# Pairs of SwiGLU chunks computed with seven products: four pairs in two rows of two in place of three single ones

## The chip, the cores and the metric

The kernel runs on one core of a Trainium2 chip. The metric is the device time of one execution in microseconds (us); less is better.

## What is computed

Two transformer blocks, one after the other, on 256 rows of 1024 features in fp32. The first block has an adaLN modulation, attention beside a convolution, and a squared-ReLU MLP with 4096 hidden features. The second has two attention branches and a SwiGLU MLP with 2816 hidden features (`D_FF_2`), 11 chunks of 256:

```python
def second_block(x, norm_mix, w_in, w_up_a, w_up_b, w_out, norm_ffn, w_gate, w_up, w_down, norm_final):
    ...
    x = x + merged @ w_out[layer]
    h = rmsnorm(x, norm_ffn[layer])
    x = x + (jax.nn.silu(h @ w_gate[layer]) * (h @ w_up[layer])) @ w_down[layer]
    return rmsnorm(x, norm_final)
```

The change touches the line with `silu`, and what is prepared for it earlier.

## The kernel before, in words

**Precision.** A product in fp32 is made of three fp32r products: of an operand, the high part H is its rounding to fp32r and the low part L the rest. PE runs H x WH, H x WL and L x WH into one bank (`part`, lines 570 to 572). A *unit* is 1 MB of weights, 128 x 2048, brought by one or two DMAs of SP's queue into one of seven slots `W32[0..6]`. ACT writes its high halves WH (`hi()`, line 1247, two instructions for a unit) and DVE its low halves WL (`lo()`, line 1791, two instructions). WL lies in the same bytes as W32. Both engines go through all units in one order, that of the list `units`; SP loads them in the order of `loads`. The queue of every engine is written out by hand, and an engine that waits holds up what stands behind it.

**The SwiGLU MLP.** The 256 rows are two blocks of 128 (`tb`), the 1024 features two halves. For one chunk, PE makes gate and up side by side, 256 + 256 columns (`up2`), for each `tb` two units of 12 matmuls. ACT takes the silu, DVE multiplies with up into `hid` (line 1800), PE transposes it (`hid_turn2`), ACT and DVE split it into HH and HL, and PE adds its product with w_down in banks 0 to 3 (`down2`). `GROUPS` lists chunks and pairs of chunks; `PAIRS = (2, 5, 8)` makes pairs of 2 and 3, 5 and 6, 8 and 9, and chunks 0, 1, 4, 7 and 10 are single.

**A pair.** Here gate and up of 512 columns for two row blocks and two halves of the features are a 2 x 2 product of blocks, made with seven products of 12 matmuls in place of eight. Four of the seven have a sum of blocks of x as one operand (`FS`, split into `FH` and `FL`; formed once by `form`, `form_hi`, `form_lo`) and four a difference of weight blocks. PE runs them in the order 1 to 7 (`begin`, `rest`, `quad_sum`): 1 (bank 4), 2 (bank 5), the down products of the group before for one `tb`, 3 (bank 6), those for the other `tb`, 4 (bank 5), 5 (bank 6), 6 (bank 4), 7 (bank 6). Between them DVE adds up banks and earlier sums (*first* to *fifth sum*, `quad_group` in `vector_program`; they write `g1b` and `quad_g1`), each raising the semaphore `quad`. The fourth product waits for the first sum, the fifth for the second and the seventh for the third, because the bank must have been read:

```python
        w.wait_ge(S["quad"], 5 * q + 2)
        quad_sum(g, 4, 3, 6, False)
        ...
        w.wait_ge(S["quad"], 5 * q + 3)
        part(by["gu", g][6], m.AH, m.AL, 4, 1, 6, False, True, "gu_mm", n_ready(2, 1), onto=True)
```

**Weight differences.** They come in two ways. *In place* (pairs not in `STORED`): DVE subtracts one unit in its slot from another (`make(g, 0)` to `make(g, 3)`, two instructions of 1024 elements each), before their low halves are made. *Stored*: four steps bring a quarter of the up and gate blocks each into a free place in SBUF (POOL, `blocks_in`), DVE makes the four differences (`kept_sums`, four instructions of 512 elements), and POOL writes them to DRAM (`kept_sums` in `pool_program`), from where SP later loads them as units. `STEPS` says how many steps there are in each of three phases and `SUMS_AT` at which place of DVE's queue they stand: places 0 to 6 are in the first block's MLP, 7 in the projections of the second block. Before, pair 2 is stored and pairs 5 and 8 are in place. `DN_ORDER`, `GU_AT`, `QUAD_AT` and the like turn the order into the semaphore values that the waits use.

## Time and profile before

| | |
|---|---|
| median of 3 runs | 718.48 us (718.40 to 718.58) |
| the profiled execution | 718.42 us |
| its span in the profile | 716.3 us |
| PE busy | 706.7 us, 99% |
| DVE busy | 574.6 us, 80% |
| ACT busy | 429.9 us, 60% |
| DMA | 163.76 MB, 229 GB/s |
| the SwiGLU MLP | from about 541 us to the end |

Start times in the trace are from the start of the span. The time of an execution is 2.1 us over its span. Ends of matmuls are modelled and overlap the next start, so PE's pace is read from start to start. In the rows, "x4" merges four instructions of one kind, and the brackets give the idle time of the engine before them and what ended it.

### The profile page before, as it was taken

What the parts mean: (1) busy time and instruction counts of PE and PEld (TensorE: products, weight loads), DVE (VectorE), ACT (ScalarE), POOL (GpSimd) and SP (SyncE); (2) the same over time, 40 slices, a digit from 0 to 9 for tenths busy, and PEclk for the clock granted to TensorE, in tenths of its full rate; (3) what the DMA queues carried; (4) which work ended last, traced back from release to release, by engine and by line L of the source; (5) the groups of instructions that cost most, each with busy time, mean ns of one, the idle gap of its engine ahead of it and who ended that gap; (6) DMA issues with size and microseconds to landing.
All of it is one profiled execution on the core that took longest, in us unless ns stands there. A gap on an engine that the chain in (4) does not pass through costs nothing.

```text
span 716.3 us, 9684 instructions
## 1 busy us (share of the span) xinstructions
PE 706.7 (99%) x3710; PEld 565.7 (79%) x3710; DVE 574.6 (80%) x972; ACT 429.9 (60%) x704; POOL 34.5 (5%) x55
## 2 busy tenths in 40 slices
PE   8999999999999999999999999999999999999996
PEld 4678885578888888888888777777888888888885
DVE  4789999899677868686998799855857789888883
ACT  3477658996745635646545677767447654754652
POOL 1030012001100100000010000000000000000000
PEclk9999999999999999999999999999999999999999
DMA  9996939617778975747538533336463894976901
GB/s 368 414 374 222 389 102 358 230 59 262 272 246 311 337 281 203 258 154 291 164 113 295 209 118 118 118 130 214 128 234 128 315 329 169 332 258 227 354 2 59
DMA packets 72109, 163.76 MB, mean 229 GB/s; under 512 B 4272, under 2 KB 15536, under 8 KB 70528
## 3 DMA queue, kind: packets, MB, share of 16 engines
q1 hardware_dynamic: 68016, 149.47, 58.8%
q0 software_dynamic: 3760, 13.42, 5.2%
q8 instruction: 29, 0.48, 0.3%
q10 hardware_dynamic: 288, 0.27, 0.1%
q14 instruction: 16, 0.13, 0.1%
HBM read 157.90 MB, written 5.24 MB: 228 GB/s over the span
## 4 chain that ended last, share of the span: by engine, by line
PE 95%; issue 1%; DVE 1%; ACT 1%; POOL 0%; POOLq 0%; DVEq 0%
PE bank L570 23%; PE bank L572 23%; PE bank L571 23%; PE bank L915 6%; PE bank L552 5%; PE bank L913 3%; PE bank L589 1%; PE bank L644 1%; PE bank L652 1%; PE bank L647 1%; PE bank L1047 1%; PE bank L1069 1%; PE bank L753 1%; PE bank L629 1%; PE bank L775 1%
## 5 line engine op out<-in xcount | busy, mean ns | idle before, releaser
L1791 DVE TENSOR_TENSOR WL<-W,WH 128x1024 fp32r<-128x1024 f32 (+2 forms) x240 | 270.4, 1172 | 25.6 <-ACT WH L1247 25.2
L1247 ACT ACTIVATE WH<-W 128x1024 fp32r<-128x1024 f32 (+2 forms) x240 | 228.6, 1013 | 63.4 <-DMA W<-in_w_mlp 38.1
L570 PE MATMUL bank<-WH,AHL 128*128 128x512 f32 (+1 forms) x420 | 165.2, 393 | 0.0
L572 PE MATMUL bank<-WH,AHL 128*128 128x512 f32 (+1 forms) x420 | 162.0, 386 | 0.0
L571 PE MATMUL bank<-WL,AHL 128*128 128x512 f32 (+1 forms) x420 | 161.8, 385 | 0.0
L570 PEld LDWEIGHTS bank<-WH,AHL 128*128 128x128 f32 x420 | 78.9, 188 | 18.2 <-issue 3.2
L572 PEld LDWEIGHTS bank<-WH,AHL 128*128 128x128 f32 x420 | 78.9, 188 | 16.2
L571 PEld LDWEIGHTS bank<-WL,AHL 128*128 128x128 f32 x420 | 79.1, 188 | 14.7
L570 PE MATMUL bank<-WH,HH 128*128 128x512 f32 (+1 forms) x218 | 84.8, 389 | 0.0
L572 PE MATMUL bank<-WH,HL 128*128 128x512 f32 (+1 forms) x218 | 84.5, 388 | 0.0
L571 PE MATMUL bank<-WL,HH 128*128 128x512 f32 (+1 forms) x218 | 84.4, 387 | 0.0
L915 PE MATMUL bank<-AHL,WH 128*128 128x512 f32 x168 | 60.5, 398 | 0.0
L913 PE MATMUL bank<-AHL,WL 128*128 128x256 f32 x192 | 50.0, 281 | 0.0
L572 PEld LDWEIGHTS bank<-WH,HL 128*128 128x128 f32 x218 | 40.9, 188 | 8.5
L571 PEld LDWEIGHTS bank<-WL,HH 128*128 128x128 f32 x218 | 41.0, 188 | 8.3
L570 PEld LDWEIGHTS bank<-WH,HH 128*128 128x128 f32 x218 | 40.9, 188 | 8.0
L913 PEld LDWEIGHTS bank<-AHL,WL 128*128 128x128 f32 x192 | 36.3, 189 | 2.0
L915 PEld LDWEIGHTS bank<-AHL,WH 128*128 128x128 f32 x168 | 31.6, 188 | 6.7
L1806 DVE SCALAR_TENSOR_TENSOR cacc<-hp,vec,cacc 128x256 f32<-128x256 f32 x88 | 36.0, 478 | 0.2
L436 POOL TENSOR_TENSOR stat<-stat 128x1 f32<-128x1 f32 x12 | 10.1, 845 | 444.3 <-DVE stat L1815 401.8
L1255 ACT ACTIVATE HH<-bank 128x512 fp32r<-128x512 f32 (+1 forms) x20 | 8.9, 487 | 24.4 <-PE bank L552 24.4
L1800 DVE TENSOR_TENSOR W<-W,W 128x1024 f32<-128x1024 f32 x16 | 18.8, 1215 | 0.0
(311 smaller groups left out, 978.5 us busy)
## 6 DMA issues: line engine op xcount, KB each, us to landing
W<-in_w_mlp SPq DMA_DIRECT2D x32, 1024.0 KB, 5.9
W<-in_w_in SPq DMA_DIRECT2D x24, 1024.0 KB, 5.5
W<-in_w_down SPq DMA_DIRECT2D x11, 1024.0 KB, 5.3
W<-in_w_ada SPq DMA_DIRECT2D x10, 1024.0 KB, 8.3
WX<-in_w_ada SPq DMA_DIRECT2D x10, 1024.0 KB, 10.2
W<-in_w_up SPq DMA_DIRECT2D x9, 1024.0 KB, 6.2
W<-in_w_out SPq DMA_DIRECT2D x8, 1024.0 KB, 5.3
W<-in_w_gate SPq DMA_DIRECT2D x8, 1024.0 KB, 5.8
```

The costliest lines, as they stand in the source:

```text
L436: e.tensor_tensor(m.stat[:, 40 + i:41 + i], m.stat[:, 24 + i:25 + i], m.stat[:, 94:95], ALU.pow).then_inc(S["rstd"], 1)
L552: ins = e.transpose(bank[b][:, c * 128:c * 128 + 128], src, m.ident[:, :])
L570: e.matmul(po, hs, wh[:, k, c0:c0 + cw], start=first and k == 0, stop=False, skip_group_check=onto)
L571: e.matmul(po, hs, wl[:, k, c0:c0 + cw], start=False, stop=False, skip_group_check=onto)
L572: ins = e.matmul(po, ls, wh[:, k, c0:c0 + cw], start=False, stop=last and k == unit.nk - 1, skip_group_check=onto)
L913: ins = e.matmul(bank[4 + j][:, 0:256], wl[:, k, js], m.AH[:, 4 * i + k, :], start=False, stop=False)
L915: ins = e.matmul(both, wh[:, k, js], m.AHL[:, :, 4 * i + k, :], start=False, stop=i == 1 and k == 3)
L1247: e.activation(m.WH[unit.slot][:, c], m.W32[unit.slot][:, c], ACT.Copy).then_inc(S["w_hi"], 1)
L1255: e.activation(o, i, ACT.Copy, scale=scale).then_inc(S[sem], 1)
L1791: e.tensor_tensor(m.WL[unit.slot][:, c], m.W32[unit.slot][:, c], m.WH[unit.slot][:, c].bitcast(F32), ALU.subtract).then_inc(S["w_lo"], 1)
L1800: e.tensor_tensor(o, a, b, op).then_inc(S[sem], 1)
L1806: e.scalar_tensor_tensor(o, a, scalar, b, op0, op1).then_inc(S[sem], 1)
```

## The change

- `PAIRS` becomes (2, 4, 7, 9): the pairs (2, 3), (4, 5), (7, 8) and (9, 10), with 0, 1 and 6 single. There is one group fewer (`NG` is 7). The first pair of each two in a row is made in place, the second is stored.
- Eight steps of stored sums in place of four: one at each of places 0 to 6 (the first phase of POOL), one at place 7 (the second).
- `NEAR` lists pairs that another pair follows. In them ACT and DVE split two units of the next pair ahead of time, in a new order within the group (`quad_group` in both programs).
- The last group is a pair; PE moves half of the down products of the pair before behind its seventh product, and `down2_last` has two units.

```diff
-PAIRS = (2, 5, 8)
-STORED = (2,)
-STEPS = (4, 0, 0)
-SUMS_AT = (1, 0, 1, 0, 0, 0, 2, 0, 0, 0, 0, 0, 0)
+PAIRS = (2,4,7,9)
+STORED = (4,9)
+STEPS = (7,1,0)
+SUMS_AT = (1,1,1,1,1,1,1,1,0,0,0,0,0)
...
+NEAR = [g for g in range(NG - 1) if GROUPS[g][1] and GROUPS[g + 1][1]]
...
     def down2_last():
...
+        g = NG - 1
         for n, (c0, cw) in enumerate(LAST[1]):
-            part(by["dn", NG - 1][0], m.HH[(NG - 1) % 2], m.HL[(NG - 1) % 2], 0, 1, (1, 4, 5)[n], n > 0, True, "dn_mm",
-                 lambda k: ("hid_lo", 16 + 2 * NG), c0, cw)
+            for i, unit in enumerate(by["dn", g]):
+                part(unit, m.HH[g % 2], m.HL[g % 2], 2 * i, 1, (1, 4, 5)[n], n > 0 and i == 0, i == 1, "dn_mm",
+                     lambda k: ("hid_lo", 16 + 2 * NG), c0, cw)
...
         quad_sum(g, 2, 1, 6, True)
-        down2(g - 1, 1, False, False)
+        if g < NG - 1:
+            down2(g - 1, 1, False, False)
         w.wait_ge(S["quad"], 5 * q + 1)
...
+    rest(NG - 1)
+    hid_turn2(NG - 1, 0)
     down2(NG - 2, 1, False, False, (0,))
     down2(NG - 2, 1, False, True, (1,))
+    down2(NG - 1, 0, False, True, (0,))
+    hid_turn2(NG - 1, 1)
+    down2(NG - 1, 0, False, True, (1,))
     down2_last()
```

On ACT, in `quad_group`, and on DVE, in `quad_group` (the bodies of the named steps are as before):

```diff
-        hi(5)
-        hi()
+        near, final = g in NEAR, g == NG - 1
+        hi(4 if g - 1 in NEAR else 5)
+        hi(2 if near else 1)
...
         if made:
             make(g, 2)
         lo()
+        if g == 2:
+            form_lo(2)
+            form_lo(3)
+        first_sum()
         if made:
             make(g, 3)
         lo()
...
         if near:
+            lo()
+            second_sum()
+            lo(4)
+            third_sum()
+            fourth_sum()
+            lo()
+            hidden(0)
+            fifth_sum()
+            lo()
+            hidden(1)
             hid_lo2(g, 0)
+            hid_lo2(g, 1)
...
+        else:
+            second_sum()
+            lo(2)
+            third_sum()
             lo()
+            fourth_sum()
...
```

**DVE at the opening of pair (2, 3).** The first row multiplies the second row block of chunk 0 with its silu (`hid0`), the last is the low part of chunk 1's hidden rows or just before it. `W32_n` is slot n, `WL_n` and `WH_n` its low and high halves, FL the low parts of the sums of x, HL those of the hidden rows. Before:

```order
L1800 TENSOR_TENSOR hid0_164<-bank5,rel1_171 128x256
L2126 TENSOR_TENSOR HL0_168<-bank7,HH0_166 128x2x128
L1791 TENSOR_TENSOR WL_5_60<-W32_5_54,WH_5_66 128x1024 x2
L1791 TENSOR_TENSOR WL_2_57<-W32_2_51,WH_2_63 128x1024 x2
L1800 TENSOR_TENSOR hid1_165<-bank1,rel1_171 128x256
L2126 TENSOR_TENSOR HL0_168<-bank6,HH0_166 128x2x128
L1800 TENSOR_TENSOR FL0_220<-FS0_216,FH0_212 128x512
L1800 TENSOR_TENSOR FL1_221<-FS1_217,FH1_213 128x512
L1800 TENSOR_TENSOR FL2_222<-FS2_218,FH2_214 128x512
L1800 TENSOR_TENSOR FL3_223<-FS3_219,FH3_215 128x512
L1791 TENSOR_TENSOR WL_3_58<-W32_3_52,WH_3_64 128x1024 x2
```

and with the change:

```order
L1799 TENSOR_TENSOR hid0_164<-bank5,rel1_171 128x256
L2125 TENSOR_TENSOR HL0_168<-bank7,HH0_166 128x2x128
L1799 TENSOR_TENSOR W32_2_51<-W32_2_51,W32_5_54 128x1024 x2
L1790 TENSOR_TENSOR WL_5_60<-W32_5_54,WH_5_66 128x1024 x2
L1799 TENSOR_TENSOR hid1_165<-bank1,rel1_171 128x256
L2125 TENSOR_TENSOR HL0_168<-bank6,HH0_166 128x2x128
L1799 TENSOR_TENSOR W32_3_52<-W32_3_52,W32_2_51 128x1024 x2
L1799 TENSOR_TENSOR FL0_220<-FS0_216,FH0_212 128x512
L1799 TENSOR_TENSOR FL1_221<-FS1_217,FH1_213 128x512
L1790 TENSOR_TENSOR WL_2_57<-W32_2_51,WH_2_63 128x1024 x2
L1790 TENSOR_TENSOR WL_0_55<-W32_0_49,WH_0_61 128x1024 x2
L2125 TENSOR_TENSOR HL1_169<-bank7,HH1_167 128x2x128
```

Two makes (W32_2 and W32_3 as outputs) have come in, and the low passes of slots 2 and 0 stand behind them; FL2 and FL3 have moved back.

**DVE from there to the third quad sum of pair (2, 3).** The rows that read bank5 or bank6 into g1b are the first, second and third sum. Before:

```order
L2126 TENSOR_TENSOR HL1_169<-bank7,HH1_167 128x2x128
L2126 TENSOR_TENSOR HL1_169<-bank6,HH1_167 128x2x128
L1791 TENSOR_TENSOR WL_0_55<-W32_0_49,WH_0_61 128x1024 x2
L1800 TENSOR_TENSOR g1b_74<-bank5,quad_g1_228 128x512
L1791 TENSOR_TENSOR WL_1_56<-W32_1_50,WH_1_62 128x1024 x2
L1800 TENSOR_TENSOR g1b_74<-bank6,quad_g1_228 128x512
L1791 TENSOR_TENSOR WL_4_59<-W32_4_53,WH_4_65 128x1024 x2
L1791 TENSOR_TENSOR WL_5_60<-W32_5_54,WH_5_66 128x1024 x2
L1800 TENSOR_TENSOR g1b_74<-bank6,g1b_74 128x512
```

and with the change (ahead of these rows stand the second HL1 row, the make of W32_1 and the low pass of slot 3):

```order
L1799 TENSOR_TENSOR FL2_222<-FS2_218,FH2_214 128x512
L1799 TENSOR_TENSOR FL3_223<-FS3_219,FH3_215 128x512
L1799 TENSOR_TENSOR g1b_74<-bank5,quad_g1_228 128x512
L1799 TENSOR_TENSOR W32_5_54<-W32_4_53,W32_5_54 128x1024 x2
L1790 TENSOR_TENSOR WL_4_59<-W32_4_53,WH_4_65 128x1024 x2
L1790 TENSOR_TENSOR WL_5_60<-W32_5_54,WH_5_66 128x1024 x2
L1799 TENSOR_TENSOR g1b_74<-bank6,quad_g1_228 128x512
L1790 TENSOR_TENSOR WL_6_210<-W32_6_209,WH_6_211 128x1024 x2
L1790 TENSOR_TENSOR WL_1_56<-W32_1_50,WH_1_62 128x1024 x2
L1790 TENSOR_TENSOR WL_2_57<-W32_2_51,WH_2_63 128x1024 x2
L1790 TENSOR_TENSOR WL_3_58<-W32_3_52,WH_3_64 128x1024 x2
L1799 TENSOR_TENSOR g1b_74<-bank6,g1b_74 128x512
```

Between the first and the second sum there is a make and two low passes where there was one low pass; between the second and the third there are four low passes where there were two.

## Rows read from the trace of the kernel before

**Rows 1.** The page, busy us (share of the span) of all engines, instructions.

```profile
PE 706.7 (99%) x3710; PEld 565.7 (79%) x3710; DVE 574.6 (80%) x972; ACT 429.9 (60%) x704; POOL 34.5 (5%) x55
```

**Rows 2.** The page, the chain that ended last, by engine.

```profile
PE 95%; issue 1%; DVE 1%; ACT 1%; POOL 0%; POOLq 0%; DVEq 0%
```

**Rows 3.** Windows: stretch, its length, busy us of each engine (instructions), granted clock, DMA.

```profile
564.00:592.00 28.00, 28.00 (x127) 23.20 (x126) 21.52 (x23) 19.00 (x21) 0.00 (x0) 1.00 0.94 343
612.00:640.00 28.00, 28.00 (x129) 23.24 (x128) 24.83 (x26) 19.03 (x22) 0.00 (x0) 1.00 0.96 339
```

**Rows 4.** Timeline of PE in pair (2, 3): start, us, line, op; fourth, sixth, seventh product.

```profile
575.31 0.39 PE L570 MATMUL bank<-WH,FH 128*128 128x512 f32 x1
...
580.75 0.39 PE L570 MATMUL bank<-WH,AHL 128*128 128x512 f32 x1
...
583.47 0.39 PE L570 MATMUL bank<-WH,AHL 128*128 128x512 f32 x1
```

**Rows 5.** Timeline of DVE, pair (2, 3); in brackets the idle time before.

```profile
551.79 0.42 DVE L2126 TENSOR_TENSOR HL<-bank,HH 128x256 fp32r<-128x256 f32 x1
552.67 4.63 DVE L1791 TENSOR_TENSOR WL<-W,WH 128x1024 fp32r<-128x1024 f32 x4 [0.46 <-ACT WH L1247]
557.22 0.42 DVE L1800 TENSOR_TENSOR hid<-bank,rel 128x256 f32<-128x256 f32 x1
...
557.88 2.49 DVE L1800 TENSOR_TENSOR FL<-FS,FH 128x512 fp32r<-128x512 f32 x4
...
566.20 2.36 DVE L1791 TENSOR_TENSOR WL<-W,WH 128x1024 fp32r<-128x1024 f32 x2 [2.90 <-ACT WH L1247]
...
572.79 0.69 DVE L1800 TENSOR_TENSOR g1b<-bank,quad_g 128x512 f32<-128x512 f32 x1 [1.35 <-PE bank L572]
...
580.95 0.69 DVE L1800 TENSOR_TENSOR g1b<-bank,g1b 128x512 f32<-128x512 f32 x1 [2.93 <-PE bank L572]
```

**Rows 6.** SP's issue of a load; the page's median us from issue to landing.

```profile
547.30 0.34 SPq L409 DMA_DIRECT2D W<-sums  x1
...
W<-in_w_up SPq DMA_DIRECT2D x9, 1024.0 KB, 6.2
...
W<-sums SPq DMA_DIRECT2D x4, 1024.0 KB, 5.1
```

**Rows 7.** Timeline of DVE, pair (5, 6), first to third quad sum.

```profile
616.14 0.68 DVE L1800 TENSOR_TENSOR g1b<-bank,quad_g 128x512 f32<-128x512 f32 x1
616.74 2.35 DVE L1800 TENSOR_TENSOR W<-W,W 128x1024 f32<-128x1024 f32 x2
619.01 2.35 DVE L1791 TENSOR_TENSOR WL<-W,WH 128x1024 fp32r<-128x1024 f32 x2
621.28 0.68 DVE L1800 TENSOR_TENSOR g1b<-bank,quad_g 128x512 f32<-128x512 f32 x1
...
628.60 0.69 DVE L1800 TENSOR_TENSOR g1b<-bank,g1b 128x512 f32<-128x512 f32 x1 [2.10 <-PE bank L572]
```

**Rows 8.** Timeline of PE, pair (5, 6), start of the seventh product.

```profile
631.12 0.39 PE L570 MATMUL bank<-WH,AHL 128*128 128x512 f32 x1
```

**Rows 9.** Timeline of DVE in the first MLP: a step of sums, a wait.

```profile
232.34 2.62 DVE L1800 TENSOR_TENSOR sums<-sums 128x512 f32<-128x512 f32 x4
...
259.24 2.36 DVE L1791 TENSOR_TENSOR WL<-W,WH 128x1024 fp32r<-128x1024 f32 x2 [4.90 <-ACT WH L1247]
```

**Rows 10.** Timeline of PE, first and last of the 12 narrow matmuls.

```profile
708.75 0.28 PE L570 MATMUL bank<-WH,HH 128*128 128x256 f32 x1
...
710.06 0.28 PE L572 MATMUL bank<-WH,HL 128*128 128x256 f32 x1
```

**Rows 11.** Windows after the last matmul; the granted clock is behind the engines.

```profile
711.00:714.00 3.00, 0.00 (x0) 0.00 (x0) 1.29 (x4) 1.14 (x3) 0.54 (x1) 1.00 0.02 8
714.00:715.00 1.00, 0.00 (x0) 0.00 (x0) 0.00 (x0) 0.00 (x0) 0.00 (x0) 0.83 1.02 389
715.00:716.30 1.30, 0.00 (x0) 0.00 (x0) 0.00 (x0) 0.00 (x0) 0.00 (x0) 0.50 0.26 93
```

More of the change, by code:

```diff
@@ L474, in kept_sums @@
             s = sum(STEPS[:phase]) + i
+            if phase == 2 and i == 1:
+                power(10)
             w.wait_ge(S["made"], 4 * s + 4)
@@ L1713, in quad_group @@
         e.activation(m.rel[1][:, :], m.g1[:, :], ACT.Silu).then_inc(S["silu"], 1)
-        if not GROUPS[g + 1][1]:
+        if near:
+            hi()
+            hid_hi2(g, 0)
+            hi()
+        elif not final:
             hi(2)
-        for tb in range(2):
-            hid_hi2(g, tb)
-        if GROUPS[g + 1][1]:
-            hi(2)
+            hid_hi2(g, 0)
+        hid_hi2(g, 1)
     silu_gate(0, 0)
@@ L2563, in quad_group, with product, first_sum, second_sum @@
         q = quads.index(g)
-        made, following, near = in_place(g), in_place(g + 1), GROUPS[g + 1][1]
+        made, near, final = in_place(g), g in NEAR, g == NG - 1
+        following = not final and in_place(g + 1)
+        def product(n):
+            w.wait_ge(S["gu_mm"], QUAD_AT[g] + n)
+        def first_sum():
+            product(2)
+            w.wait_ge(S["quad_act"], q + 1)
+            if q:
+                w.wait_ge(S["hid2"], HID_AT[quads[q - 1], 1])
+            tt(m.u1, bank[5][:, :], m.g1[:, :], ALU.add, "quad")
+        def second_sum():
+            product(3)
+            tt(m.u0, bank[6][:, :], m.g1[:, :], ALU.add, "quad")
+        def third_sum():
+            product(5)
+            tt(m.u1, bank[6][:, :], m.u1, ALU.add, "quad")
+        def fourth_sum():
+            product(4)
+            w.wait_ge(S["quad"], 5 * q + 2)
+            tt(m.u0, bank[5][:, :], m.u0, ALU.add, "quad")
+        def fifth_sum():
+            product(7)
+            tt(m.g1[:, :], bank[6][:, :], m.g1[:, :], ALU.add, "quad")
+        def hidden(tb):
+            w.wait_ge(S["hid_turned"], 4 + 2 * (g - 2) + 2)
+            w.wait_ge(S["silu"], SILU_AT[g, tb])
+            w.wait_ge(S["quad"], 5 * q + 4)
+            tt(m.hid[g % 2][:, tb, :], (m.u0, m.u1)[tb], m.rel[tb][:, :], ALU.mult, "hid2")
         if made:
@@ L2661, in vector_program @@
                 hid_lo2(g, tb)
[L2662 to L2666 removed]
+    quad_group(NG - 1)
     def last(tb):
```

127 lines of the change are left out of this document (42 added, 85 removed).

## The prediction

> **What bounds the kernel now.** I read the busy shares first: PE is busy for 706.7 of 716.3 us and DVE for 80% of it [rows 1]. Then the chain of waits: 95% of it is PE, and no other engine has over 1% [rows 2]. So a microsecond of PE work is worth a microsecond, and work on another engine costs nothing until PE waits for it. The stage windows show how near that is: PE fills all of 564 to 592 and of 612 to 640 at a granted clock of 1.00, while DVE has 21.5 and 24.8 us of 28 to do [rows 3]. Last I read the queues of PE and DVE side by side there, because DVE works in the order in which it is written, and that order is what the change rewrites.
>
> A product (12 matmuls of 512 columns) takes PE 2.72 us: the fourth of pair (2, 3) starts at 575.31, the sixth 24 matmuls later at 580.75, the seventh at 583.47 [rows 4]. That is 0.2267 us for a matmul. From start to start, an FL row takes DVE 0.60 us (four rows from 557.88 with 2.49 us to the last end) and a small row of 256 elements 0.33 us (two from 557.22 to 557.88) [rows 5]. A quad sum takes 616.14 to 616.74, 0.60 us; a difference of two weight blocks (two W rows, "a make") 616.74 to 619.01, 2.27 us; a low pass (one unit, two WL rows) 619.01 to 621.28, also 2.27 us [rows 7].
>
> **What it removes.** The fourth pair makes 7 products of what were 8. In matmuls of the whole program it is 18 fewer of 512 columns and 12 more of 256, since the narrow last rows now have two units. The first and the last of the 12 there now start at 708.75 and 710.06, so they come 0.119 us apart [rows 10]. 18 x 0.2267 - 12 x 0.119 = **-2.65 us** of PE, all on the path. PE's tail after its last matmul keeps its form: 0.
>
> **Sums kept in DRAM, eight steps in place of four.** A step is four DVE rows, 2.6 us [rows 9]. The added ones stand at the end of a chunk of the first MLP, where DVE idles: in one of them it waits 4.90 us before the low pass at 259.24 [rows 9], and in each chunk it waits for ACT or PE somewhere. The block that they delay is used by PE a chunk later. POOL's added copies (eight loads of half a unit, four stores) are queued behind nothing that PE needs; the last of the first seven is issued before the power of the next norm, as now. The eighth, in the second block's projections, delays DVE by 2.6 us ahead of ropes and relu rows for which it waits on ACT. I cost all of it at nothing; if that cover were gone it would be at most 2.6 us for a step. Extra DMA: 8 MB through the sums and 3 MB of units. I count 0 to 1 us for both.
>
> **DVE's queue in pair (2, 3), the first place.** Before, this pair is stored, so DVE has no makes in it. It waits for others four times between 552.13 and the third sum: 0.46, 2.90, 1.35 and 2.93 us [rows 5]. Now the pair is made in place, so four makes stand there, and because another pair follows, four low passes stand between the second and the third sum in place of two, and one more before the second. The order of both places is shown above. I add it up from the first make. DVE is ready for it at 552.13; its block is loaded by the transfer issued at 547.30, and a W<-in_w_up lands after a median of 6.2 us, the sums now loaded there after less (the page has 5.1). I take 5.4, so 552.7; from both ends it is 552.4 to 553.5 [rows 6]. Behind it stand
> - 4 makes x 2.27 = 9.1
> - 10 low passes x 2.27 = 22.7
> - 4 FL x 0.60 = 2.4
> - 4 small rows (one product with the gate, three HL) x 0.33 = 1.3
> - 3 quad sums x 0.60 = 1.8
>
> together 37.3 us. **The third sum is done at 590.0.** The same by difference: it is done at 581.55 now; four makes and three low passes more are 15.9, the four waits that vanish are 7.6, which gives 589.8. The seventh product waits for this sum and PE wants it at 583.47, so PE loses 6.5 us here. Earlier waits in the pair are part of that: the fourth product waits some 1.0 us for the low half of its unit, the fifth 1.3 us for the second sum (done at 580.3), and the gap before the seventh is 590.0 - 585.8 = 4.2 us.
>
> ACT doesn't add to it: the high halves of the four units (2.0 us each, behind a load that may start only when the forms are split, at 572.3) run just ahead of the low passes. Behind the seventh product the hidden rows come as a chain over DVE and ACT (fourth sum, low, hidden, fifth sum, silu, high and low of one unit, hidden, HL), which ends some 0.4 us after PE has done its two next products and a transpose. First place: **+6.9 us** (bounds 5 and 8: the landing, and whether ACT or a late load holds a low pass).
>
> **Pair (7, 8), the second place.** It stands behind a single chunk as the pair (5, 6) does now, so it can be read in that one's times. The first sum starts at 616.14, the make runs to 619.01; with two low passes in place of one, the second sum is done at 624.15, 1.5 us before PE wants it. Four low passes end at 633.2, the third sum at 633.8. PE wants the seventh product at 631.12 [rows 8], and now the sum starts at 628.60 after a wait of 2.10 us [rows 7]. PE loses 2.7 us, and 0.3 at the hidden rows: **+3.0 us** (bounds 1.5 and 4).
>
> **Pairs (4, 5) and (9, 10)** are stored and keep the short order. DVE has already done two of their low passes, and before the second sum PE has two chunks' down products (5.4 us) to do. In the last pair the second half of those moves behind the seventh product, so the fourth product follows the third directly; its unit and first sum are ready by then. 0, and up to 1 us if one is late.
>
> **Sum:** -2.65 + 6.9 + 3.0 = +7.25. The profiled execution took 718.42 us (2.1 around its span), so 725.7. The median of the runs shown is 718.48, which is the same within 0.1.
>
> A clock effect is weighed against it. The trace grants 1.00 (2.4 GHz) all through PE's work; after the last matmul ends at 710.34 [rows 10] the granted share is still 1.00 over 711 to 714, 0.83 over 714 to 715 and then 0.50, so it fell to 1.2 GHz some 4.3 us into the idle time [rows 11]. My gap of 4.2 us is just short of that. The Trainium skill ("TensorE: Matmul & The Clock Gate", section "Why this matters for your kernels") says that an idle gap of PE between bursts of matmuls puts it back to half its clock. By the trace the sum stays; by that rule it would be the rival below.
>
> **The rivals.**
> 1. The clock falls in the gap before the seventh product. For it: the 4.3 us of rows 11 against 4.2 here, with error on both. Against it: the waits of 1.0 and 1.3 us before it split the loss. If PE then works at half clock for as long as that same 4.3 us, it does 2.15 us less: 725.7 + 2.2 = **727.9 us**. Chance 0.17.
> 2. Only one place costs much: DVE catches up in the second pair, since the idle 2.10 us and the waits of 1 us for ACT there go, or the first is nearer its low bound. 725.7 - 3.0 = 722.7, with the first at its bound 720.8: **722 us**. Chance 0.15.
> 3. **Faster.** The four low passes are hidden. This holds if the second sum is done 9.1 + 0.6 us before PE wants the seventh product, that is by 573.8 in the first pair and 621.4 in the second. In the first pair PE gives its operand just in time for that (now the second sum starts at 572.79, after DVE has waited 1.35 us for PE), so the order is right for a DVE that is on time, and then nothing is lost: 718.4 - 2.65 = **715.8 us**. By my sum DVE is 6.5 and 2.7 us late, since it must fit the makes in too; rows 5 show only 7.6 us of idle time to take 15.9. Chance 0.09.
> 4. The gain and one small loss cancel (only the second pair's 3.0): 718.8, **no change**. Chance 0.04.
>
> **The numbers.** Forecast (725.7, both places, clock kept): 0.55. 0.2% (1.4 us) is about what a measurement here can tell from no change. Faster has 0.09, same 0.04, slower 0.87. The range takes in the forecast with its bounds (722.5 to 729), rival 1 and most of rival 2: 721 to 729.5.
>
> **What would show it.** In the changed profile DVE should have no wait between its first make (near 552.7) and the third sum of pair (2, 3). PE should stand still for some 1.0, 1.3 and 4.2 us before the fourth, fifth and seventh product, then 2.7 us before the seventh of pair (7, 8), both ended by DVE's write of g1b. Before 552 the traces should agree within 0.5 us, with 32 rows of sums in place of 16. Wrong is the forecast if the third sum of pair (2, 3) ends before 584 with PE not waiting, if PE waits for a DMA or ACT in its place, or if time is lost in the first MLP. A granted clock under 1.00 after the gap would be rival 1.

## The result and the profile after

The changed kernel takes **729.73 us** (median of 4 runs, 729.33 to 730.63) against 718.53 us (4 runs, 718.4 to 718.81): ratio **1.0152**, 95% interval 1.014 to 1.0165. The profiled execution took 729.45 us, its span is 727.6 us. The forecast was 725.7 us with a range of 721 to 729.5. The direction and the places hold, 4 us are missing from the sum, and the median lies 0.2 us above the top of the range (the ratio, 1.0152 times the 718.48 us of before, gives 729.4).

The page of the changed kernel, answering to [rows 1, 2]: its span, its busy engines, the chain by engine, and the group of matmuls that waited most.

```profile
span 727.6 us, 9712 instructions
...
PE 709.1 (97%) x3704; PEld 566.1 (78%) x3704; DVE 593.6 (82%) x995; ACT 436.4 (60%) x707; POOL 43.2 (6%) x67
...
PE 82%; DVE 8%; DMA 5%; ACT 3%; issue 1%; SPq 0%; POOLq 0%; POOL 0%; DVEq 0%
...
L571 PE MATMUL bank<-WH,AHL 128*128 128x512 f32 (+1 forms) x400 | 159.0, 397 | 6.9 <-DVE g1b L1799 6.9
```

In the kernel before, 95% of the chain was PE. Now 8% is DVE, and the matmuls of line 571 with AHL as an operand (the first of each three) stood still for 6.9 us for DVE's write of g1b, a quad sum. That is the wait that the forecast put in both places. DVE's queue in pair (2, 3), answering to [rows 5]; columns as there:

```profile
552.71 2.36 DVE L1799 TENSOR_TENSOR W<-W,W 128x1024 f32<-128x1024 f32 x2 [0.26 <-DMA W<-in_w_up]
...
572.35 0.68 DVE L1799 TENSOR_TENSOR g1b<-bank,quad_g 128x512 f32<-128x512 f32 x1
...
579.76 0.68 DVE L1799 TENSOR_TENSOR g1b<-bank,quad_g 128x512 f32<-128x512 f32 x1
580.37 9.15 DVE L1790 TENSOR_TENSOR WL<-W,WH 128x1024 fp32r<-128x1024 f32 x8
589.45 1.27 DVE L1799 TENSOR_TENSOR g1b<-bank,g1b 128x512 f32<-128x512 f32 x2
...
595.62 0.69 DVE L1799 TENSOR_TENSOR quad_g<-bank,quad_g 128x512 f32<-128x512 f32 x1 [2.03 <-PE bank L573]
```

The first make starts at 552.71 (forecast 552.7). From there to the third sum no row of DVE has a wait in brackets. The two sums at 589.45 take 0.60 us each from start to start, so the third is done at 590.05 (forecast 590.0). PE in the same place, and at the second place, answering to [rows 4, 8]:

```profile
576.58 0.47 PE L571 MATMUL bank<-WH,FH 128*128 128x512 f32 x1 [0.64 <-DVE WL L1790]
...
580.50 0.50 PE L571 MATMUL bank<-WH,FH 128*128 128x512 f32 x1 [0.93 <-DVE g1b L1799]
...
585.84 0.39 PE L573 MATMUL bank<-WH,AHL 128*128 128x512 f32 x1
590.18 0.80 PE L571 MATMUL bank<-WH,AHL 128*128 128x512 f32 x1 [3.95 <-DVE g1b L1799]
590.77 0.63 PE L572 MATMUL bank<-WL,AHL 128*128 128x512 f32 x1
...
598.18 0.60 PE L553 MATMUL bank<-ident,hid 128*128 128x128 f32 x4
...
671.05 0.39 PE L573 MATMUL bank<-WH,AHL 128*128 128x512 f32 x1
674.39 0.80 PE L571 MATMUL bank<-WH,AHL 128*128 128x512 f32 x1 [2.96 <-DVE g1b L1799]
674.99 0.63 PE L572 MATMUL bank<-WL,AHL 128*128 128x512 f32 x1
```

Start to start, less the 0.227 us of a matmul that runs, PE lost 0.8 us before the fourth product, 1.1 before the fifth, 4.1 before the seventh, and 3.1 before the seventh of pair (7, 8). Now look at the length of the first matmul behind each long gap: 0.80 us, and 0.59 us to the start of the next, where 0.39 and 0.227 are usual. The 24 matmuls from 590.18 to 598.18 take 8.00 us, where 24 take 24 x 0.2267 = 5.44. PE works at half clock there, for a part of the time. The windows over both places say so too (columns as in [rows 3]; the granted clock stands behind POOL):

```profile
564.00:592.00 28.00, 22.48 (x92) 17.39 (x91) 28.00 (x30) 16.58 (x18) 0.00 (x0) 0.94 0.86 325
588.00:596.00 8.00, 5.82 (x15) 4.62 (x16) 5.97 (x8) 0.75 (x1) 0.00 (x0) 0.57 0.56 216
673.00:678.00 5.00, 3.60 (x10) 2.89 (x11) 4.81 (x6) 0.96 (x2) 0.00 (x0) 0.66 0.59 216
```

DVE has 28.0 of 28 us to do where it had 21.5 [rows 3]. A mean clock of 0.57 over 8 us is (1 - 0.57) x 8 / 0.5 = 6.9 us at 1.2 GHz; 0.66 over 5 us is 3.4 us. Before, both windows were at 1.00.

To compare kernels I cut PE's time at the same transposes in every trace: the hidden rows near 206 us, the norm's first turning near 350 and near 527, the first hidden row of the second MLP near 550, and the end of the last matmul. All in us:

| kernel | to 206 | 206 to 350 | 350 to 527 | norm, 527 to 550 | MLP stage, to PE's end |
|---|---|---|---|---|---|
| before | 206.20 | 143.00 | 177.05 | 23.58 | 160.51 |
| after | 206.56 | 143.00 | 176.94 | 23.58 | 171.58 |

PE's end comes 11.32 us later, and 11.07 of them lie in the last stage. Most of the rest is the opening to 206 us (0.36), which differs by more than that between traces (below). From 206 to 350, where six of the eight steps stand, both kernels take 143.00 us.

### The profile page after: what moved, and what is told of

Its sections match the earlier page's. It is cut to its first block, busy times and chain, and to the rows that moved or that the text cites. A ratio compares the mean times of both kernels' runs of the same rounds, so it can differ in the third digit from the quotient of the medians.

```text
span 727.6 us, 9712 instructions
## 1 busy us (share of the span) xinstructions
PE 709.1 (97%) x3704; PEld 566.1 (78%) x3704; DVE 593.6 (82%) x995; ACT 436.4 (60%) x707; POOL 43.2 (6%) x67
## 4 chain that ended last, share of the span: by engine, by line
PE 82%; DVE 8%; DMA 5%; ACT 3%; issue 1%; SPq 0%; POOLq 0%; POOL 0%; DVEq 0%
PE bank L571 20%; PE bank L573 20%; PE bank L572 20%; PE bank L916 5%; DVE WL L1790 5%; PE bank L553 4%; PE bank L914 3%; DMA W<-in_w_up 2%; DMA W<-in_w_in 2%; DVE W L1799 2%; DMA WX<-in_w_ada 1%; ACT WH L1249 1%; PE bank L590 1%; PE bank L1048 1%; PE bank L1070 1%
## 5 line engine op out<-in xcount | busy, mean ns | idle before, releaser
L1790 DVE TENSOR_TENSOR WL<-W,WH 128x1024 fp32r<-128x1024 f32 (+2 forms) x246 | 276.7, 1172 | 16.3 <-ACT WH L1249 16.2
L1249 ACT ACTIVATE WH<-W 128x1024 fp32r<-128x1024 f32 (+2 forms) x246 | 234.4, 1014 | 77.2 <-DMA W<-in_w_mlp 36.5
L571 PE MATMUL bank<-WH,AHL 128*128 128x512 f32 (+1 forms) x400 | 159.0, 397 | 6.9 <-DVE g1b L1799 6.9
L573 PE MATMUL bank<-WH,AHL 128*128 128x512 f32 (+1 forms) x400 | 155.5, 389 | 0.0
L572 PE MATMUL bank<-WL,AHL 128*128 128x512 f32 (+1 forms) x400 | 155.4, 389 | 0.0
L571 PEld LDWEIGHTS bank<-WH,AHL 128*128 128x128 f32 x400 | 76.2, 191 | 25.6 <-DVE g1b L1799 7.8
L573 PEld LDWEIGHTS bank<-WH,AHL 128*128 128x128 f32 x400 | 76.0, 190 | 15.8
L572 PEld LDWEIGHTS bank<-WL,AHL 128*128 128x128 f32 x400 | 76.2, 190 | 14.2
L571 PE MATMUL bank<-WH,FH 128*128 128x512 f32 x64 | 25.4, 396 | 1.6 <-DVE g1b L1799 0.9
L572 PE MATMUL bank<-WL,FH 128*128 128x512 f32 x64 | 25.0, 390 | 0.0
```

The lines of the kernel that those rows point to most:

```text
L571: e.matmul(po, hs, wh[:, k, c0:c0 + cw], start=first and k == 0, stop=False, skip_group_check=onto)
L572: e.matmul(po, hs, wl[:, k, c0:c0 + cw], start=False, stop=False, skip_group_check=onto)
L573: ins = e.matmul(po, ls, wh[:, k, c0:c0 + cw], start=False, stop=last and k == unit.nk - 1, skip_group_check=onto)
L1249: e.activation(m.WH[unit.slot][:, c], m.W32[unit.slot][:, c], ACT.Copy).then_inc(S["w_hi"], 1)
L1790: e.tensor_tensor(m.WL[unit.slot][:, c], m.W32[unit.slot][:, c], m.WH[unit.slot][:, c].bitcast(F32), ALU.subtract).then_inc(S["w_lo"], 1)
```

## The experiments

Two questions were open: whether DVE's order alone makes the loss, place by place, and how much of it is the clock. A third came up on the way: whether the 2.65 us of saved matmuls can be kept. The stage lengths of each kernel's profiled execution stand in one table behind the last run.

**1. The low passes behind the third sum.** The edit, in DVE's `quad_group`: two of the four low passes between the second and the third sum move behind it, one after each hidden row.

```diff
         if near:
             lo()
             second_sum()
-            lo(4)
+            lo(2)
             third_sum()
             fourth_sum()
             lo()
             hidden(0)
+            lo()
             fifth_sum()
             lo()
             hidden(1)
             hid_lo2(g, 0)
+            lo()
             hid_lo2(g, 1)
```

> The change with one thing altered: in a pair that another pair follows, DVE makes the low halves of the next pair's first two units after the fourth sum and after the first hidden row, and no longer before the third sum. Theory (order): the third sum of pair (2, 3) comes 4.5 us earlier, PE waits only some 0.8 and 1.1 us before the fourth and fifth product, not before the seventh, and not in pair (7, 8); the clock stays at 1.00. About 718.3 us. Rival (DVE is simply short of time): the wait moves on to the hidden transposes and the next pair's first products, 721 to 723 us.

Measured: 719.4 us (718.8 to 720.21, 10 runs), ratio 1.0009 (0.9999 to 1.0018). Ten of the eleven microseconds are gone with three lines of order, makes and steps unchanged. The theory of order holds, though its 718.3 us were 1.1 too low. Both gaps before a seventh product went, and the clock stayed at 1.00. DVE's third sum of the first place now starts at 586.08, with two low passes ahead of it. That is 3.4 us earlier, and 4.7 (expected 4.5) if one takes off that this execution was 1.3 us later at its first hidden row of the second MLP:

```profile
580.94 0.68 DVE L1799 TENSOR_TENSOR g1b<-bank,quad_g 128x512 f32<-128x512 f32 x1
581.54 4.62 DVE L1790 TENSOR_TENSOR WL<-W,WH 128x1024 fp32r<-128x1024 f32 x4
586.08 1.28 DVE L1799 TENSOR_TENSOR g1b<-bank,g1b 128x512 f32<-128x512 f32 x2
```

What is left are the waits of 0.8 and 1.1 us before the fourth and fifth product and 0.6 us at the hidden rows (596.03 and 596.92), which the theory hadn't.

**2. The gaps filled with matmuls.** The change as it is, with 16 and 11 matmuls of 512 columns into an unused bank just ahead of the wait for the third sum. Their result is used by nothing.

```diff
         frees(4, ("silu", SILU_AT[g, 0]))
+        if g in NEAR:
+            take(7)
+            for _ in range((16, 11)[q > 0]):
+                e.matmul(bank[7][:, :], m.AH[:, 4, 0:128], m.WH[by["gu", g][5].slot][:, 0:512], start=True, stop=True)
         w.wait_ge(S["quad"], 5 * q + 3)
```

> The change, with 16 and 11 matmuls of 512 columns put into bank 7, which nobody reads then, before PE's wait for the third sum in the two places. DVE's order is untouched. Theory (half clock is a loss of its own, some 2.5 and 1.4 us): granted clock 1.00 throughout and about 725.8 us. Rival (the loss is DVE's lateness alone, the clock only shows it): 729.7 us.

Measured: 726.1 us (725.92 to 726.52, 4 runs), ratio 1.0101 (1.0086 to 1.0116): 3.6 us less than the change, although PE has 27 matmuls more to do. The windows of this run:

```profile
588.00:596.00 8.00, 7.68 (x34) 6.03 (x33) 6.67 (x8) 2.60 (x4) 0.00 (x0) 1.00 0.77 273
673.00:678.00 5.00, 5.00 (x25) 4.08 (x24) 3.35 (x5) 1.66 (x3) 0.00 (x0) 1.00 0.53 165
```

So the clock's share is 3.6 us in the medians and 171.58 - 167.84 = 3.74 us in the stage. It is a price of its own, on top of the waits. The rows of the change give the same: the 24 matmuls behind a gap take 8.00 us in the first place and 6.95 in the second (674.39 to 681.34), and 5.6 behind a gap after which the clock stayed up (experiment 6, 591.71 to 597.29). That is 2.4 and 1.35 us, together 3.75. The Trainium skill ("TensorE: Matmul & The Clock Gate", section "Why this matters for your kernels") says that a long enough idle gap between bursts of matmuls puts PE back to half its clock; by that rule these runs agree, in gaps of 4.1 and 3.1 us.

**3. The eight steps alone.** The kernel before, with its last pair stored as well: two stored pairs, eight steps, at the change's own places. Pairs and products as before.

```diff
-STORED = (2,)
-STEPS = (4, 0, 0)
-SUMS_AT = (1, 0, 1, 0, 0, 0, 2, 0, 0, 0, 0, 0, 0)
+STORED = (2, 8)
+STEPS = (7, 1, 0)
+SUMS_AT = (1, 1, 1, 1, 1, 1, 1, 1, 0, 0, 0, 0, 0)
```

> The kernel before with pairs 2 and 8 stored and eight steps of kept sums at the same places as in the change (pair 8 no longer in place). Theory (the added steps and their DMA are hidden): 718.5 us, within 0.4. Rival (they cost something in the first MLP or in the projections): 719.5 us or more.

Measured: 718.98 us (718.25 to 719.51, 10 runs), ratio 1.0002 (0.9992 to 1.0011). The four added steps and their transfers are hidden within what the medians can tell (0.19 us apart), and the MLP stage is 160.51 us as before, to the hundredth. Not quite nothing is left of them in this execution: PE waits 0.3 us for DVE's g2b at 319.43, and 206 to 350 takes 143.41 us.

**4. Pair (2, 3) stored as well.** Takes the makes out of the first place, with the short order of experiment 1. Twelve steps: the four added ones at places 9 to 11, behind the merges of the second block and in the norm. POOL's powers for that norm now stand between its copies.

```diff
-STORED = (4,9)
-STEPS = (7,1,0)
-SUMS_AT = (1,1,1,1,1,1,1,1,0,0,0,0,0)
+STORED = (2, 4, 9)
+STEPS = (7, 1, 4)
+SUMS_AT = (1, 1, 1, 1, 1, 1, 1, 1, 0, 1, 1, 2, 0)
...
-    make(2, 0)
...
-    make(2, 1)
```

> The change with the first pair stored too (twelve steps; the last four around the output projection of the second block, where DVE has idle time) and the late low passes of e1. Theory: the makes leave DVE's queue in pair (2, 3), no wait of PE is left in either place, only the 2.65 us fewer matmuls count: about 716.3 us, faster than both. Rival (the four late steps delay the second norm or the forms): 718 us or more, with a wait before 552.

Measured: 720.19 us (719.98 to 721.13, 9 runs), ratio 1.0024 (1.0014 to 1.0034). The MLP stage took 157.92 us, 2.59 us under the kernel before: the saved matmuls are worth what the sum gave them once nothing stands in DVE's queue. But the steps cost more than that, so the expected 716.3 us failed and the rival's 718 or more holds, with the delay at the merges and not in the norm. PE's rows there:

```profile
505.60 0.60 PE L552 MATMUL bank<-ident,mrg 128*128 128x128 f32 x4
508.10 1.05 PE L552 MATMUL bank<-ident,mrg 128*128 128x128 f32 x4 [1.91 <-DVE mrg L1798]
```

The step at place 9 made DVE's merges 2.6 us late. PE lost 2.1 us (from the last of the four transposes at 505.92 to 508.10, less the 0.11 of a transpose), and the clock fell in this gap too, for 3.4 us.

**5. The steps moved.** As experiment 4, with the step of place 9 moved into the fifth chunk of the first MLP.

```diff
-STEPS = (7, 1, 4)
-SUMS_AT = (1, 1, 1, 1, 1, 1, 1, 1, 0, 1, 1, 2, 0)
+STEPS = (8, 1, 3)
+SUMS_AT = (1, 1, 1, 1, 2, 1, 1, 1, 0, 0, 1, 2, 0)
...
         lo(2)
+        if c == 4:
+            kept_sums(4, 0, 1)
```

> All four pairs' seven products, pair (2, 3) kept in DRAM too (no makes in it), short order of the low passes at both places; of the twelve sums steps the one behind the last merge of the first up projection (which in the run before held DVE up by 2.6 us, before PE's wait of 2.24 us and a spell at half clock of 1.3 us) now stands in the fifth chunk of the first MLP; the one further on and the two in the next norm stay. Theory (the saved matmuls are worth 2.65 us once neither DVE's queue nor a step stands before PE, and the step behind the merges alone made that wait): no wait of PE over 0.5 us between 500 and 690, clock 1.00 until the last matmul, 716.4 us (715.8 to 717.0), ratio 0.997. Rival A (the step further on, not the moved one, made the wait): PE still waits some 2 us near 505 and the time stays near 720. Rival B (DVE has no room for two steps in one chunk of the first MLP, 20.3 of 22.2 us being taken there in rows): PE waits up to 2.6 us between 280 and 320, 719.

Measured: 719.22 us (718.31 to 723.17, 11 runs), ratio 1.0015 (1.0003 to 1.0027). The theory (716.4 us) named one place and there were three. The wait at 505 went, as expected, but the step left at place 10 costs one too, and the first MLP has room for seven steps and not for eight (rival B, at 320):

```profile
320.65 0.50 PE L912 MATMUL bank<-AHL,WH 128*128 128x512 f32 x1 [1.62 <-DVE g2b L1798]
...
511.97 0.50 PE L570 MATMUL bank<-WH,AHL 128*128 128x512 f32 x1 [1.04 <-DVE AHL L2124]
```

**6. The change's order without makes in the first place.** As experiment 5, with `lo(4)` between the second and third sum again.

```diff
-            lo(2)
+            lo(4)
             third_sum()
...
-            lo()
             fifth_sum()
...
-            lo()
             hid_lo2(g, 1)
```

> As the run with the moved steps, but with the change's own order of the low passes (four between the second and third sum). So the first place has the four low passes without the makes, the second place has both, as in the change. Theory (a place costs what DVE's rows before the third sum are over PE's time): first place, the sum is done near 584.0 against 583.5 wanted, so PE loses 0.3 to 1.0 us there and keeps its clock; second place loses 3.1 us and 1.5 us to the half clock as in the change: 5.3 us above the run with the moved steps, 721.7 us (721 to 722.6). Rival (the four low passes in a row cost much by themselves, makes or not): PE waits 3 us or more in the first place too and loses the clock in both, 726 or more.

Measured: 726.48 us (725.44 to 729.54, 5 runs), ratio 1.0117 (1.01 to 1.0134): 7.3 us above experiment 5, not 5.3. The time is the rival's, the waits are not. Both places wait for g1b:

```profile
591.71 0.50 PE L570 MATMUL bank<-WH,AHL 128*128 128x512 f32 x1 [1.61 <-DVE g1b L1798]
...
673.57 0.61 PE L570 MATMUL bank<-WH,AHL 128*128 128x512 f32 x1 [2.87 <-DVE g1b L1798]
```

The first place loses 1.8 us with the clock kept (expected 0.3 to 1.0: I had the second sum done too early, it ends at 581.9 with DVE never idle behind 572.7). The second loses 3.0 us and the clock. The profiled execution also shows a wait of 3.0 us at 319 with a fall of the clock behind it, where experiment 5 had 1.8 us and none; the stage from 206 to 350 took 147.60 against 144.90 us. Why the same step costs more in one execution than in another was not settled.

**7. Only the second gap filled.** As experiment 2, with `if g in NEAR and q > 0` and the 11 matmuls alone.

> The change, with 11 more matmuls of 512 columns into an unused bank in the second gap alone (pair (7, 8)); their result is not used. Theory (each gap costs its own spell at half clock): the granted clock stays 1.00 from 600 to the last matmul, the first gap still has its 6.8 us at half clock, and 1.5 us of the 3.6 that both fills saved are saved: 728.3 us (727.9 to 728.6). Rival (the second fall hangs on the first, a clock that fell once falls more easily): the fill changes nothing beyond the noise or the 11 matmuls cost time, 729.5 or more, and the fall at the first place alone explains the whole 3.6.

Measured: 727.6 us (726.95 to 728.8, 4 runs), ratio 1.0131 (1.0115 to 1.0146), 2.1 us under the change where 1.5 was expected. The second place kept its clock, so its fall doesn't hang on the first. The windows tell where the rest comes from:

```profile
588.00:596.00 8.00, 6.14 (x20) 4.92 (x21) 5.96 (x8) 1.20 (x3) 0.00 (x0) 0.79 0.55 200
673.00:678.00 5.00, 4.80 (x21) 4.00 (x22) 4.21 (x6) 0.76 (x2) 0.00 (x0) 1.00 0.51 168
```

0.79 over 8 us is 3.4 us at half clock, where the change's profiled execution had 6.9 us behind the same gap of 4.1 us. The 24 matmuls behind the gap take 7.18 us here and 8.00 there, so what a fall costs differs between executions by 0.8 us, and that is the other part of the 2.1.

**8. The last four steps on POOL.** As experiment 4, but POOL makes the subtractions of the last four steps itself, in `kept_sums` of its own program, and DVE has the change's eight.

```diff
+        for to, a, b, at_least in ((g0, u0, g0, 0), (u0, u1, u0, 1), (u1, u1, g0, 2), (g1, g1, u1, 3)):
+            if at_least:
+                w.wait_ge(S["pool_tiles"], n + at_least)
+            e.tensor_tensor(to, a, b, ALU.subtract).then_inc(S["pool_tiles"], 1)
```

> All four pairs' seven products, pair (2, 3) kept in DRAM too, short order at both places; the first eight sums steps are DVE's at the change's own eight places, the last four (the four subtractions each) are done by POOL, which has the blocks from the second block's attention on and idles there. So DVE has no row more than in the kernel before up to 552. Theory (the saved matmuls are worth 2.65 us where nothing stands in DVE's queue for them): PE has no wait over 0.5 us from 200 to 690, clock 1.00 until the last matmul, 716.0 us (715.4 to 716.6), ratio 0.9965. Rival A (POOL's rows slow DVE's down, or hold up the norm's powers, which stand between them): DVE's rows between 497 and 545 get longer or stat rows wait over 1 us more for POOL, and PE waits 1 to 4 us there: 717 to 720. Rival B (the stores land late for the units of pair (2, 3)): a wait for a DMA at 552 to 565, 717 or more.

Measured: 721.58 us (721.26 to 723.07, 5 runs), ratio 1.0047 (1.0033 to 1.0061). Rival A, and dearer than it was put. POOL's and DVE's rows in this trace:

```profile
510.75 7.46 POOL L477 TENSOR_TENSOR sums<-sums 128x512 f32<-128x512 f32 x4
...
503.00 1.07 DVE L1812 TENSOR_TENSOR mrg<-mrg,mt 128x512 f32<-128x512 f32 x1
504.00 2.35 DVE L1803 TENSOR_TENSOR WL<-W,WH 128x1024 fp32r<-128x1024 f32 x2
506.27 0.68 DVE L1812 TENSOR_TENSOR mt<-bank,gb 128x512 f32<-128x512 f32 x1
506.98 0.69 DVE L1812 TENSOR_TENSOR mrg<-mrg,mt 128x512 f32<-128x512 f32 x1
...
510.31 5.06 DVE L1803 TENSOR_TENSOR WL<-W,WH 128x1024 fp32r<-128x1024 f32 x2
515.29 0.68 DVE L1812 TENSOR_TENSOR mt<-bank,gb 128x512 f32<-128x512 f32 x1
```

The low pass at 504.00, between two of POOL's steps, takes its usual 2.35 us. The one at 510.31, beside POOL's subtractions, takes 5.06. A step takes POOL 5.5 to 7.5 us, and beside it a low pass takes DVE up to twice its time. Not every row of DVE is slowed: mrg<-mrg,mt, with both inputs in SBUF, takes 1.07 us while POOL subtracts (503.00; its step there runs from 496.39 to 503.5) and 0.69 while it doesn't (506.98), and mt<-bank,gb, with one input in a bank, takes 0.68 either way (506.27, 515.29). PE lost 1.7 us before 507.73 and 2.1 before 530.61. The Trainium skill ("SBUF — State Buffer", section "SBUF: two separate sides") says that a DVE instruction with two inputs in SBUF and a POOL instruction that reads SBUF contend for one shared pair of ports, which the first to start holds for its whole length while the other blocks. By that rule the trace agrees in which rows are slowed: a low pass reads W and WH from SBUF.

**9. The same with the change's order.** As experiment 8, with `lo(4)` as in experiment 6.

> As the run with POOL's steps, but with the change's own order of the low passes at both places (four between the second and third sum). Theory (the order costs by itself where the second sum is not done 9.8 us before PE wants the seventh product, makes or not): as in the earlier run with this order, the first place loses 1.8 us with the clock kept, the second 3.0 us and 1.4 us by the half clock, hidden rows 0.2: 6.4 us above the run with POOL's steps, 722.4 us (721.6 to 723.2). Rival (the 1.8 us came from DVE's steps in the norm ahead, which made it late at 552): no loss over 0.4 us in the first place, 720.9 or less.

Measured: 728.97 us (727.13 to 730.07, 4 runs), ratio 1.0141 (1.0127 to 1.0155), 7.4 us above experiment 8 (expected 6.4). In the MLP stage it is 164.65 - 157.94 = 6.7 us: 1.8 in the first place with the clock kept, 2.9 and the clock in the second. DVE had no step in the norm here, and the first place lost the same 1.8 us. So that loss is the order's own. The norm is longer too (25.25 us against 24.57); the clock fell there in a gap of 2.3 us.

**10. The steps in DVE's waits.** All twelve on DVE again: seven in the first MLP, a second one in the projections ahead of the fifth indexer row (DVE waits 4.06 us for ACT there), one split around the low rows of the second merge, two in the norm. One thing more differs from experiment 5: POOL issues its reload of the sums buffer behind the power of the norm, there ahead of it.

```diff
-STEPS = (8, 1, 3)
-SUMS_AT = (1, 1, 1, 1, 2, 1, 1, 1, 0, 0, 1, 2, 0)
+STEPS = (7, 2, 3)
+SUMS_AT = (1, 1, 1, 1, 1, 1, 1, 1, 1, 0, 1, 2, 0)
...
     for h in range(8):
+        if h == 4:
+            kept_sums(8)
...
+    last_rows = sums_rows(10)
+    next(last_rows)
     merged_lo(1)
+    next(last_rows, None)
```

> All four pairs' seven products, pair (2, 3) kept in DRAM too, short order at both places, all twelve sums steps on DVE again, each where DVE waits anyway: seven in the first MLP at the change's places; two in the second block's projections, the second of them moved in front of the fifth indexer row, where DVE waits 4.06 us for ACT; one split around the low rows of the second merge (three rows in a wait of 1.64 us, one behind it); two in the next norm, where DVE waits 1.71 and 4.18 us. Theory (a step of 2.6 us is free where DVE waits as long, and the saved matmuls are then worth 2.65 us): no wait of PE over 0.5 us from 200 to 690 but up to 0.5 near 527, clock 1.00 until the last matmul, 716.4 us (715.8 to 717.1), ratio 0.997. Rival A (the split step's last row and the norm's two steps make DVE late for the norm): PE waits 1 to 2 us between 527 and 552, 717.5 to 718.5. Rival B (the saved matmuls give less than 2.65 us, something else fills in, as the runs so far that had all seven-product pairs never came under the kernel before): 718.5 or more with no wait of PE to show for it.

Measured: 718.77 us (717.77 to 719.85, 11 runs), ratio 1.0 (0.9991 to 1.0009). The moved steps cost nothing now (350 to 527: 176.94 us), but the norm took 25.63 us in place of 23.58, near rival A. The second step in it waited for its blocks, which POOL had reloaded late, and PE for DVE behind it:

```profile
534.19 2.62 DVE L1798 TENSOR_TENSOR sums<-sums 128x512 f32<-128x512 f32 x4 [2.02 <-DMA sums<-in_w_gate]
...
537.47 0.50 PE L570 MATMUL bank<-WH,AHL 128*128 128x512 f32 x1 [1.14 <-DVE AHL L1798]
```

**11. The reload ahead of the norm's power.** In POOL's `kept_sums` the two are swapped, nothing else.

```diff
-            if phase == 2 and i in (0, 2):
-                power(10 + i // 2)
             if i + ahead < STEPS[phase]:
                 blocks_in(phase, i + ahead)
+            if phase == 2 and i in (0, 2):
+                power(10 + i // 2)
```

> The run with the steps in the gaps, but POOL issues the reload of the sums buffer before the norm's power and not behind it (in the run before, the second step in the norm waited 2.02 us for that load, so DVE was late by 1.5 to 2 us and the stage from the norm's first turning to the first hidden row took 25.6 us against 23.6). Theory (that wait was what ate the gain): the load lands some 1.4 us earlier, the stage takes 23.6 to 24.3 us, everything else as in the run before: 717.2 us (716.5 to 717.9), ratio 0.998. Rival (the power, now behind the reload, comes late and holds the norm up as much): stat rows wait over 1 us more for POOL, PE waits at the norm's first turning near 527, and the time stays within 718.3 to 719.3.

Measured: 718.54 us (717.63 to 720.13, 11 runs), ratio 1.0001 (0.9992 to 1.001). The step's wait shrank, and the norm's own row now waits a microsecond longer for POOL. The norm takes 24.17 us, as the theory said, and the time is the rival's:

```profile
526.52 0.48 DVE L1801 TENSOR_SCALAR S<-X,stat 128x512 f32<-128x512 f32 x1 [1.69 <-POOL stat L437]
...
532.65 2.62 DVE L1798 TENSOR_TENSOR sums<-sums 128x512 f32<-128x512 f32 x4 [0.49 <-DMA sums<-in_w_gate]
```

The profiled execution is the fastest of the eleven, 717.63 us, with PE done at 709.16 against 710.34 us before. The median doesn't show that gain. In experiment 5 the reload also stood ahead of the power and the norm took 23.58 us; what makes the 0.59 between them stays open.

**12. The short order in the first place alone.** As experiment 1, in pair (2, 3) only; pair (7, 8) keeps the change's order.

> The change, with the short order of the low passes (two before the third sum, the others behind it) in pair (2, 3) alone; pair (7, 8) keeps the change's order. Theory (the two places add up, each with its own spell at half clock): the first place costs what it did with the short order in both (waits of 0.8, 1.1 and 0.6 us, clock 1.00), the second what it does in the change (3.1 us and 1.5 us by the half clock): the stage from the first hidden row to the last matmul takes 161.0 + 4.7 = 165.7 us (in the change 171.6), 724.0 us in all (723.3 to 724.7). Rival (a late first place is what makes the second late, or lets its clock fall): the second place loses under 1.5 us, 720 to 721.5.

Measured: 724.76 us (722.21 to 725.41, 4 runs), ratio 1.0074 (1.0049 to 1.0098). The MLP stage took 165.69 us where 165.7 was expected. The first place had the waits of experiment 1; the second is as in the change, in time and in clock:

```profile
669.13 0.50 PE L571 MATMUL bank<-WH,AHL 128*128 128x512 f32 x1 [2.69 <-DVE g1b L1799]
```

The stages of all kernels, cut as above:

| kernel | to 206 | 206 to 350 | 350 to 527 | norm | MLP stage |
|---|---|---|---|---|---|
| 1 low passes late | 207.51 | 143.00 | 177.30 | 23.58 | 161.04 |
| 2 both gaps filled | 206.75 | 143.00 | 177.17 | 23.58 | 167.84 |
| 3 eight steps alone | 206.44 | 143.41 | 176.95 | 23.58 | 160.51 |
| 4 pair (2, 3) stored | 206.32 | 143.00 | 180.91 | 23.57 | 157.92 |
| 5 steps moved | 206.20 | 144.90 | 178.30 | 23.58 | 157.94 |
| 6 as 5, change's order | 206.66 | 147.60 | 178.46 | 23.58 | 164.79 |
| 7 second gap filled | 206.25 | 143.00 | 177.09 | 23.58 | 169.33 |
| 8 steps on POOL | 206.46 | 143.00 | 181.15 | 24.57 | 157.94 |
| 9 as 8, change's order | 207.09 | 143.01 | 181.65 | 25.25 | 164.65 |
| 10 steps in waits | 206.60 | 143.58 | 176.94 | 25.63 | 157.93 |
| 11 reload first | 206.81 | 143.00 | 177.25 | 24.17 | 157.93 |
| 12 first place short | 206.91 | 143.57 | 176.89 | 23.58 | 165.69 |

## Why the prediction was right in its places and short in its sum

The stage lengths split the 11.07 us without a remainder. From the kernel before to those with seven products in four pairs and nothing late, 160.51 to 157.93: **-2.58**. From there to experiment 1, which has the makes in pair (2, 3), 157.93 to 161.04: **+3.11**. To experiment 12, which adds the change's order in the second place: **+4.65**. To the change, which adds it in the first: **+5.89**. Experiment 2 says that 3.74 of these are the clock: by the rows behind the two gaps 2.4 in the first place and 1.35 in the second.

- **Saved matmuls, forecast -2.65.** Right: -2.57 to -2.59 in five traces.
- **Eight steps at no cost, forecast 0 (0 to 1).** Right, within its bound: experiment 3, and 143.00 us from 206 to 350 in both kernels. In three other traces with the same seven steps in the first MLP (experiments 3, 10 and 12) this stage takes 0.4 to 0.6 us more, with a wait of PE for DVE's g2b of 0.3 to 0.5 us near 320. The forecast leaned on a wait of 4.90 us in one chunk [rows 9]. So it was near the edge, and experiment 5 shows that an eighth step in the first MLP is no longer free.
- **First place, forecast +6.9.** The mechanism and the moment were right: no wait of DVE from 552.71, the third sum done at 590.05, PE's waits 0.8, 1.1 and 4.1 us against 1.0, 1.3 and 4.2. By stages the place costs 3.11 + 5.89 = 9.0 us. Less the clock's 2.4, that is 6.6 us, against the 6.9 forecast.
- **Second place, forecast +3.0.** The gap was 3.1 us. With the clock the place costs 4.65, without it 3.3.
- **Pairs (4, 5) and (9, 10), forecast 0.** Right: PE loses nothing over 0.2 us in them.
- **The clock, forecast 0 in the sum.** This is the step that failed. "My gap of 4.2 us is just short of that" set the gap against the 4.3 us in which the clock stayed up after the last matmul [rows 11], a single case with no work behind it. The other traces end in the same idle time, and there the clock stayed up for anything from 2.0 us (experiment 3) to 5.0 us (experiment 12), so the 4.3 was no bound even for that end:

```profile
712.00:713.00 1.00, 0.00 (x0) 0.00 (x0) 0.27 (x2) 0.11 (x1) 0.54 (x1) 0.96 0.00 0
713.00:714.00 1.00, 0.00 (x0) 0.00 (x0) 0.64 (x1) 0.61 (x1) 0.00 (x0) 0.50 0.00 0
```

In this trace (experiment 3) the last matmul ends at 710.89, and by the 0.96 the clock fell at 712.9. The forecast also weighed the first place alone: no rival had a fall in the second. The clock fell in both gaps, of 4.1 and 3.1 us, and experiment 12 lost it in one of 2.9. Rival 1 was the true case for its place, and its price of 2.2 us was near the 2.4 lost there. With the same price for a fall in both places the sum would have been 725.7 + 2 x 2.15 = 730.0.

That the range reached up to 729.5 is not because it foresaw this. Its highest rival stood at 727.9; the rest of its width came from the bounds of the two places, which were met near their middle. That the time fell beside its edge is luck.

Without the clock the forecast stands: the stage of experiment 2 is 7.33 us over the kernel before, where the terms gave 7.25, and its median is 726.1 us against 725.7.

The other rivals fell. Rival 2 (only one place costs much) is excluded by the two waits and by experiment 12; rivals 3 and 4 by the time. The condition that rival 3 named, a second sum done 9.7 us ahead of the seventh product, does decide: it is missed in both places, makes or not (experiments 6 and 9: 1.8 us in the first without makes).

**Is there a version that beats both?** The gain of 2.58 us in the MLP stage is there in five kernels, but the units that must then be made ahead need four more steps, and each of those had to be paid for elsewhere. The two best, experiments 10 and 11, are level with the kernel before: ratios 1.0 and 1.0001. By the table, 10 gives back 2.05 us in the norm and 0.58 in the first MLP, and 11 gives back 0.59 in the norm and 0.2 from 350 to 527. Both, and every kernel with twelve steps, also give back 0.65 us behind the last matmul, where the table ends: from its end to the end of the span it is 6.6 us with twelve steps (experiments 4 to 6 and 8 to 11) and 5.96 to 5.99 us with four or eight. POOL's closing DRAIN takes 5.0 us there, 4.1 with eight steps and 3.1 in the kernel before. With twelve it ends 6.4 us behind the last matmul, where SP is done at 5.8, and so ends the program. The profiled execution of 11 is 0.8 us faster than the one of before, its median is not. The runs of 11 spread over 2.5 us and those of the kernel before, on the same chip, over 0.8 us. What makes that spread stays open. It isn't the opening alone, which differs by up to 1.3 us between traces (206.20 to 207.51) with no pattern by kernel.

## What to carry to other kernels

Add up the queue of the engine that produces, row by row, from the first row that the change moves to the row that the bottleneck waits for. Four low passes in a row were 9.1 us of queue between two sums, and no busy share shows that. Give every gap of PE that you forecast at 2 us or more a second price for the clock, at each place apart, and don't take one survived idle time as the bound. A step that is hidden says nothing of the next one: look for the wait that it is to fill, with its length, and for the load that must land before it.
